# A hybrid decoder step on one core: group norm of a scan's head pair deferred into the next head pair, low parts of the weights split on VectorE, and the last matmul job cut in two halves

## The reference, cut to what matters

```python
# RWKV-7, 8 heads of 64; state S per head, one step per token:
S = S * decay + (S @ (-kk)) (kk * a) + v k      # outer products
y = S @ r
# then per head: group norm, bonus, gate
y = (y - mean(y)) / sqrt(var(y) + GN_EPS) * ln_g + ln_b
o = (y + sum(r * k * r_k) * v) * g
...
x = x + relu(x @ W_up) ** 2 @ W_down            # squared-ReLU MLP
y_out = rmsnorm(x, norm_final_g)
```

## Time and profile before

| | us |
|---|---|
| median of three runs | 1272.91 |
| the three runs | 1270.98, 1272.91, 1279.83 |
| the profiled execution's own time | 1272.74 |
| span of its trace, first to last instruction | 1271.1 |
| busy: PE, DVE, ACT, POOL | 1209.3, 661.1, 385.7, 181.3 |
| mean granted clock of TensorE | 0.986 |

### The profile page before, as it was taken

One profiled execution on the slowest core, in us unless ns is written; L12 is line 12 of the kernel. 1 busy time (PEld: TensorE's weight loads), 2 busy tenths in 40 slices (PEclk: granted clock), 3 DMA queues, 4 the chain that ended last, 5 costly groups with the idle time before them and its releaser, 6 DMA issues.

```text
span 1271.1 us, 26790 instructions
## 1 busy us (share of the span) xinstructions
PE 1209.3 (95%) x11356; PEld 1077.9 (85%) x11359; DVE 661.1 (52%) x1190; ACT 385.7 (30%) x743; POOL 181.3 (14%) x218
## 2 busy tenths in 40 slices
PE   7999999898999899889989999999999999999994
PEld 5777665585887888887888899999999999999994
DVE  4898778440634534544362466656554254354334
ACT  2211333343532334333333342233232122122121
POOL 0414000111442242231142200000000000000000
PEclk9999999999999999989999999999999999999997
DMA  8234533233101111201211156522222222222101
GB/s 309 80 121 151 166 114 133 80 137 117 35 19 61 60 53 62 102 11 60 96 68 36 45 189 221 199 96 71 92 75 100 80 87 101 70 97 100 67 34 71
DMA packets 39178, 122.82 MB, mean 97 GB/s; under 512 B 5282, under 2 KB 16546, under 8 KB 30482
## 3 DMA queue, kind: packets, MB, share of 16 engines
q1 hardware_dynamic: 37106, 116.01, 26.2%
q0 software_dynamic: 1952, 5.09, 1.2%
HBM read 109.18 MB, written 11.90 MB: 95 GB/s over the span
## 4 chain that ended last, share of the span: by engine, by line
PE 86%; DVE 7%; issue 2%; ACT 2%; POOL 1%; DMA 1%; SPq 0%; DVEq 0%; ACTq 0%; POOLq 0%
PE ps L1540 13%; PE ps L1543 13%; PE ps L1539 13%; PE ps L989 7%; PE ps L980 5%; PE ps L947 5%; PE ps L981 3%; PE ps L982 3%; PE ps L1283 2%; PE ps L1107 2%; PE ps L1334 1%; PE ps L987 1%; PE ps L984 1%; PE ps L1371 1%; PE ps L1347 1%
## 5 line engine op out<-in xcount | busy, mean ns | idle before, releaser
L563 ACT ACTIVATE wh<-land 128x1024 fp32r<-128x1024 f32 (+1 forms) x125 | 122.1, 977 | 360.3 <-PE ps L1543 360.3
L571 DVE TENSOR_TENSOR wl<-land,wh 128x1024 fp32r<-128x1024 f32 (+1 forms) x94 | 103.3, 1099 | 149.7 <-ACT wh L563 149.0
L980 PE MATMUL ps<-xghi,wh 128*128 128x272 f32 x464 | 151.6, 327 | 9.8 <-ACT R L1652 8.5
L1539 PE MATMUL ps<-xhi,wh 128*128 128x272 f32 x512 | 138.3, 288 | 0.0
L1540 PE MATMUL ps<-hl,wh 128*128 128x272 f32 x512 | 138.2, 289 | 0.0
L1540 PE MATMUL ps<-xlo,wh 128*128 128x272 f32 x512 | 138.2, 289 | 0.0
L1539 PE MATMUL ps<-hh,wh 128*128 128x272 f32 x512 | 138.1, 288 | 0.0
L981 PE MATMUL ps<-xlo,wh 128*128 128x272 f32 x464 | 135.1, 291 | 0.0
L982 PE MATMUL ps<-xghi,wl 128*128 128x272 f32 x464 | 134.9, 291 | 0.0
L980 PEld LDWEIGHTS ps<-xghi,wh 128*128 128x128 f32 x464 | 88.9, 192 | 23.6 <-issue 14.3
L1543 PE MATMUL ps<-xhi,wl 128*128 128x272 f32 x512 | 106.1, 288 | 0.0
(11 more groups left out here) (436 smaller groups left out, 2390.5 us busy)
## 6 DMA issues: line engine op xcount, KB each, us to landing
land<-in_slabs SPq DMA_DIRECT2D x51, 1024.0 KB, 4.8
ring<-in_slabs SPq DMA_DIRECT2D x14, 1024.0 KB, 5.4
gates<-R SPq DMA_DIRECT2D x24, 272.0 KB, 2.1
merge<-gates SPq DMA_DIRECT2D x24, 272.0 KB, 2.9
land<-in_slabs SPq DMA_DIRECT2D x12, 512.0 KB, 5.0
R<-in_kv SPq DMA_DIRECT2D x24, 128.0 KB, 2.0
pb<-in_kv SPq DMA_DIRECT2D x24, 128.0 KB, 2.0
xT<-in_xT SPq DMA_DIRECT2D x4, 544.0 KB, 6.9
```

The lines of the kernel that those rows point to most:

```text
L563: act.activation(hi, src, ACT.Copy).then_inc(s["weights_hi"], 1)
L571: dve.tensor_tensor(lo, src, hi.bitcast(F32), ALU.subtract).then_inc(s["weights_lo"], 1)
L980: pe.matmul(ps[:, b, 0:HALF], whi[:, k], hi, start=a, stop=False)
L1539: pe.matmul(ps[:, b + h, 0:HALF], whi[:, k], hi[k][:, c], start=a, stop=False)
```

## The change

1. **Group norm of pair j is deferred.** Its mean wide is put into prep of pair j+1 behind the first fill place, its centring on DVE behind that; the square on ACT and the var wide come before chunk 0 of j+1; the square root on ACT in chunk 0; reciprocal, product, scale and shift, and gate on DVE in the chunks 2, 3, 5 and 6; the gate's wide in chunk 5. Only pair 3's stays in the old place. The outputs `y_` and the bonus have buffers for each pair.
2. **Pair j+1 is begun earlier.** `ahead(j+1, 0..2)` (token mix, scan, subtractions) goes into chunk 7 and dec of pair j, the exponentials to ACT in dec, `factors(j+1)` on DVE behind the last step of dec. The differences of r are issued early on POOL.
3. **`early_lo` goes from POOL's queue to DVE's**, one behind a chunk's state or in dec, prep and gn.
4. **Budgets**: prep 5, 5, 4, 4 instead of 8, 8, 6, 8; a chunk 2, 3, 3 instead of 2, 2, 2 (5 in two places); dec 5 each; pair 3's gn 9, 13, 15. The total stays.
5. **The last down job is done one half after the other** (`split_by_half`), so that the first half's norm can start while the second is multiplied. The sum over features gives 68 partitions x 4 columns (`end_sum`, 68x1 matmuls), on which root and reciprocal are taken; `end_spread` brings it back to 128 partitions. The stores go out as four DMAs a half.
6. Small ones: a different order of the branch sources' splits, the copy of y ahead of an eviction in chunk 7, `fill("dec", j, 1)` ahead of the inverse's second step.

```diff
@@ fill_plan
-        waits += [(("prep", j, n), b) for n, b in zip((0, 1, 3, 2), (8, 8, 6, 8) if j else (8, 22, 10, 8))]
+        waits += [(("prep", j, n), b) for n, b in zip((0, 1, 3, 2), (5, 5, 4, 4) if j else (8, 22, 10, 8))]
...
-        waits += [(("chunk", NCH * j + c, n), 5 if (c, n) == (NCH - 1, 2) else 2) for c in range(NCH) for n in range(3)]
-        waits += [(("dec", j, n), 4) for n in range(5)]
-        waits += [(("gn", j, n), b) for n, b in enumerate((6, 6, 10))]
+        waits += [(("chunk", NCH * j + c, n), (5 if j and c == 4 else 2, 3, 5 if c == NCH - 1 else 3)[n]) for c in range(NCH) for n in range(3)]
+        waits += [(("dec", j, n), 5) for n in range(5)]
+    waits += [(("gn", 3, n), b) for n, b in enumerate((9, 13, 15))]
@@ early_lo
-        def early_lo(pool, n):
-
-            pool.wait_ge(s["weights_hi"], n - PARTS0 + 1)
+        def early_lo(dve, n):
+
+            dve.wait_ge(s["weights_hi"], n - PARTS0 + 1)
             src, hi, lo = split_views(n)
-            pool.tensor_tensor(lo, src, hi.bitcast(F32), ALU.subtract).then_inc(s["early_lo"], 1)
+            dve.tensor_tensor(lo, src, hi.bitcast(F32), ALU.subtract).then_inc(s["early_lo"], 1)
@@ PE, prep
                 else:
                     fill("prep", j, 0)
-                fill("prep", j, 1)
-                fill("prep", j, 3)
+                    pe.wait_ge(s["s_y_out"], j)
+                    wide(0, k_("blk"), y_[j - 1]).then_inc(s["mean"], 1)
+                    fill("prep", j, 1)
+                    pe.wait_ge(s["sstate"], j)
                 pe.wait_ge(s["rk"], j + 1)
                 wide(6, k_("blk"), L_).then_inc(s["rk_sum"], 1)
+                if j:
+                    fill("prep", j, 3)
+                    pe.wait_ge(s["yc"], j)
                 fill("prep", j, 2)
                 if j < 3:
                     fill("need", "pb", 9 + j)
-                if j:
-                    pe.wait_ge(s["oB_out"], j)
@@ PE, chunks
+                if j:
+                    pe.wait_ge(s["yc_sq"], j)
+                    wide(0, k_("blk"), var_[j - 1]).then_inc(s["var"], 1)
                 for c in range(NCH):
...
+                    if j and c == 0:
+                        fill("chunk", n, 2)
+                        pe.wait_ge(s["y_rt"], j)
                     if j < 3 and c in (0, 1, 3):
                         early(j + 1, (0, 1, 0, 2)[c])
-                    fill("chunk", n, 2)
+                    if j and c == 5:
+                        if j < 3:
+                            pe.wait_ge(s["kk_rt"], j + 2)
+                        wide(0, lora[:, 512 + P * (j - 1):512 + P * j], t13).then_inc(s["g"], 1)
+                    if not (j and c == 0):
+                        fill("chunk", n, 2)
@@ PE, dec
+                fill("dec", j, 1)
                 pe.wait_ge(s["s_inv_out"], 4 * j + 2)
                 for hh, hp, hs in HEAD:
                     mm = pe.matmul(ps[hs, 7, 0:NS], ssq[hs], sx[hs], start=True, stop=True)
                 mm.then_inc(s["s_inv"], 1)
-                fill("dec", j, 1)
@@ PE, last job
+            split_by_half(NJOB - 1, H[1], 0, range(KT))
+            split_by_half(NJOB - 1, H[1], 1, range(0, 3))
+            pe.wait_ge(s["norm_rt"], 3)
+            end_sum(0)
+            split_by_half(NJOB - 1, H[1], 1, range(3, 6))
+            end_spread(0)
+            split_by_half(NJOB - 1, H[1], 1, range(6, KT))
+            end_sum(1)
+            end_spread(1)
@@ ACT, chunk 0
                     evacs("chunk", n, 1)
+                    if j and c == 0:
+                        act.wait_ge(s["var"], j)
+                        act.activation(h2(var_[j - 1]), pair(0), ACT.Sqrt, bias=gneps, scale=1.0 / 64).then_inc(s["y_rt"], 1)
                     if j < 3 and c < 4:
                         early(j + 1, c)
@@ DVE, chunks and dec
+                    if c:
+                        for m in splits(("chunk", n - 1)):
+                            early_lo(dve, m)
                     if j < 3 and c < 7:
                         early(j + 1, c)
+                    if j and c in (2, 3, 5, 6):
+                        group_norm(j - 1, (0, 0, 1, 2, 0, 3, 4)[c])
+                    if j < 3 and c == NCH - 1:
+                        ahead(j + 1, 0)
+                        ahead(j + 1, 1)
...
+                if j < 3:
+                    ahead(j + 1, 2)
+                for n in splits(("chunk", NCH * j + NCH - 1), ("dec", j, 0)):
+                    early_lo(dve, n)
                 dve.wait_ge(s["s_inv"], 2 * j + 1)
...
+                if j < 3:
+                    factors(j + 1)
+                    dve.wait_ge(s["sstate"], j + 1)
+                    dve.tensor_copy(sdec, tA[:, SEQ + 3:TOK:4])
+                for n in splits(("dec", j, 2), ("dec", j, 4)):
+                    early_lo(dve, n)
@@ DVE, end
+            end_add(0)
+            end_inverse(0)
+            end_scale(0, range(0, 2))
+            end_add(1)
+            end_scale(0, range(2, 5))
+            end_inverse(1)
+            end_scale(0, range(5, KT))
+            end_scale(1, range(KT))
```

More of the change, by code:

```diff
@@ L290, in split_tags @@
         tags += [("chunk", NCH * j + c, 2) for c in range(NCH)]
-        tags += [("dec", j, n) for n in (0, 2, 4)] + [("gn", j, n) for n in (1, 2)]
+        tags += [("dec", j, n) for n in (0, 2, 4)]
+    tags += [("gn", 3, n) for n in range(3)]
     order = {tag: n for n, tag in enumerate(FILLS)}
@@ L480, in build @@
         AR, bt, kt_, tA, tB = cut(R, 8 * TOK, 2, TOK), slot[10], slot[11], slot[12], slot[13]
-        y_ = r_
+        y_ = [pb3[:, 4 + j, 0:TOK] for j in range(3)] + [r_]
+        bonus = [pb3[:, 8 + j, 0:TOK] for j in range(3)] + [L_]
+        kka = k__
+        var_ = [L_, L_, r_, tA]
         G = 14 * TOK
@@ L846, in _ @@
             diff(v__, 8)
+            pool.wait_ge(s["t12"], 2)
+            diff(r_, 0)
             for j in range(4):
-                if j:
[L849 to L852, removed]
                 if j == 0:
@@ L888, in _ @@
                     diff(v__, 9 + j)
+                    pool.wait_ge(s["factors"], j + 1)
+                    diff(r_, j + 1)
                 if j == 0:
@@ L1576, in _ @@
                 split_step(up0 + n, X, ks)
-            for n in range(up0 + 2, NJOB):
+            for n in range(up0 + 2, NJOB - 1):
                 kind, idx, *_ = JOBS[n]
@@ L1834, in _, with exps @@
             evacs("c", 4)
+            def exps(j):
+                act.wait_ge(s["lx"], j + 1)
+                act.activation(tA, L_, ACT.Exp).then_inc(s["exps"], 1)
+                act.activation(tB, L_, ACT.Exp, scale=-1.0).then_inc(s["exps"], 1)
+                act.activation(lw, a_, ACT.Exp).then_inc(s["exps"], 1)
+                act.activation(scf, scf, ACT.Exp).then_inc(s["exps"], 1)
             for j in range(4):
@@ L1952, in _ @@
                         square(3, xT3, TOK, idx - 25)
-            norm(3, xT3, TOK, KT - 1)
+            end = evacuated(NJOB - 1, "v")
+            for h in range(2):
+                c = slice(h * HALF, (h + 1) * HALF)
+                act.wait_ge(s["evac_v"], end + h)
+                act.wait_ge(s["norm_ss"], KT * 4 - 2)
+                act.activation(nbuf[3][0][:, (KT - 1) % 2, c], xT3[:, KT - 1, c], ACT.Square).then_inc(s["norm_sq"], 1)
+                act.wait_ge(s["norm_sum"], 3 + 2 * h)
+                act.activation(endt[0:QT, 4 * h:4 * h + 4], ps[0:QT, 4 + h, 0:4], ACT.Sqrt, bias=epsc[0:QT],
+                               scale=1.0 / D).then_inc(s["norm_rt"], 1)
         @block.vector
@@ new lines, in _ @@
+            for n in range(3, 7):
+                early(0, n)
+            for n in range(3):
+                ahead(0, n)
+            factors(0)
+            for j in range(4):
+                if j:
+                    group_norm(j - 1, 0)
+                dve.wait_ge(s["rk_sum"], j + 1)
+                dve.tensor_tensor(h2(bonus[j]), pair(6), h2(v__), ALU.mult).then_inc(s["bonus"], 1)
+                if j == 0:
+                    dve.tensor_copy(sdec, tA[:, SEQ + 3:TOK:4])
+                    early_lo(dve, PARTS0)
+                    early_lo(dve, PARTS0 + 1)
@@ L2280, in _ @@
                                       mask_bc, ALU.mult).then_inc(s["m4"], 1)
+                for n in splits(("prep", j)):
+                    early_lo(dve, n)
                 for r in range(1, 4):
@@ L2392, in _ @@
             inverse(2, TOK)
-            for n in range(job_at("up", 0), NJOB):
+            for n in range(job_at("up", 0), NJOB - 1):
                 kind, idx, *_ = JOBS[n]
```

231 lines of the change are left out of this document (143 added, 88 removed).

## The result

| | before | after |
|---|---|---|
| median, us | 1274.55 (6 runs, 1270.98 to 1279.83) | 1254.78 (6 runs, 1253.59 to 1258.55) |
| the profiled execution, us | 1272.74 | 1254.46 |
| its span, us | 1271.1 | 1252.8 |
| mean granted clock | 0.986 | 0.993 |

The ratio is 0.985 with a 95% interval of 0.983 to 0.9869: faster by 1.5%, 19.8 us between the medians. The forecast was 1253 us. Between the two profiled executions the sum had 19.4 us less, and 18.3 came.

The account below looks back on a forecast made before the run. PE, busy 95% of the span, was taken as the bound, leaving its waits to gain: from 1272.74 us, 28.8 removed, 16.4 added, 7.0 less at the end gave 1253 us, range 1243 to 1262.

Parts of the forecast that it names:

- (a): Boundaries between two pairs: PE's idle time and slower clock in three stretches go, 23.4 us less.
- (b): A chunk of pair 2: the late state behind a POOL low part, with its clock fall, goes, 3.2 us less.
- (c): Start of dec, three times: the wait goes as the copy of y moves ahead of an eviction, 2.2 us less.
- A1: First fill step behind the mean wide, three times: waits 1.6 us for a low part on DVE, 4.8 us more.
- A2: The inverse in dec: four uncovered waits of about 0.5 us and smaller ones at other steps, 2.7 us more.
- A3: Chunks 0 and 1: u waits behind the tanh's table load, 1.8 us for pairs 1 and 2, 3.9 us more altogether.
- A4, A5: Chunk ends with the z copy queued on ACT, 1.4 us more; chunk 4 of pair 0 on DVE, 0.2 us more.
- A6: PE's clock behind the new waits: two falls taken out of five long waits, 3.4 us more, bounds 0 to 8.5.
- the end: Behind the last matmul 9.7 us instead of 18.2, with 1.5 more inside the last job: 7.0 us less.
- DVE as the bound: Rival: DVE bounds the chunk loop at the state's scaling, 1287 us at 1.2 us per chunk; chance 0.03.
- the boundary did not stay: Rival: PE still stands at the pairs, only the end and a part gained, 1266 to 1269 us; chance 0.07.
- The clock at each new wait: Rival: all five long waits of A1 and A3 bring a clock fall, 1258.4 us; chance 0.14.

Follow-up runs that it names:

- e6: Changed kernel with dec's low part put ahead of the next pair's factors on DVE; 1253.55 us, ratio 0.983.
- e2: Changed kernel with the next pair's mix, scan, exponentials and factors back in prep, norm still deferred; 1267.74 us, ratio 0.9958.
- e1: Changed kernel with the low parts back on POOL, all else kept; 1262.01 us, ratio 0.9904.
- e5: Changed kernel with a one-column tanh behind the deferred norm's root in pairs 1 and 2, loading the tanh's table early; 1249.89 us, ratio 0.9806.
- e3: Changed kernel with the last job, final norm and stores as before the change; 1258.95 us, ratio 0.9886.
- e4: Changed kernel with 15 of the low parts, those between chunk states, computed twice on DVE; 1259.08 us, ratio 0.9879.
- e7: Changed kernel with dec's second fill place dealt three steps ahead of the inverse's second step and two behind; 1256.53 us, ratio 0.9857.
- e8: Changed kernel with the three edits of e5, e6 and e7 together; 1248.06 us, ratio 0.9788.
- e9: Changed kernel with the edits of e5 and e6, dec's fill steps back behind the inverse's second step, and DVE's order in dec changed; 1245.39 us, ratio 0.9771.

## Why the prediction was right

The time was forecast within 2 us, and most terms by place and size. Against the profiled executions, in us:

| term | forecast | measured | from |
|---|---|---|---|
| (a) boundaries | -23.4 | -22.0 | idle 15.4 gone; three stretches at lower clock, 1.6, 3.4 and 1.6 |
| (b) chunk of pair 2 | -3.2 | -3.2 | no such wait |
| (c) start of dec | -2.2 | -2.2 | no such wait |
| A1 | +4.8 | +4.1 | 3 x 1.35, after against e6; the waits show 3 x 1.1 |
| A2 | +2.7 | +2.3 | 4 x 0.58 |
| A3 | +3.9 | +3.5 | 2 x 1.76 |
| A4, A5 | +1.6 | +1.6 | 5.5 less 3.5, less the 0.4 of before |
| A6 clock | +3.4 | +3.4 | two falls, both at A3 |
| the end | -7.0 | -5.0 | 11.0 + 2.2 against 18.2 |
| sum | -19.4 | -17.5 | the spans: -18.3 |

That the sums agree so closely has some luck in it. What (a) and the end give back was taken 3.4 us too high, and A1 to A3 cost 1.5 us less than was taken, so that the errors work against each other. The stretch up to the scan was 1.4 us shorter, of which 0.7 is a wait for a load, and another 0.6 us or so stand against it that no row names.

*The mechanism of (a)* is shown for the early start: with it undone (e2), the wait for the factors comes back at all three boundaries. Its size was taken too high, because the work was counted as bare matmuls; each change between scan and fill steps costs PE a little more (the 0.49 us of the fill step behind the wide in the earlier trace rows against 0.29 inside a run), and that stays. No run undoes the norm's deferral alone, or the budgets alone; what each of them does to the boundaries is argued from the order of the queues. (b) and (c) went, but no run takes them apart either, and that (b) went because the low parts left POOL is not shown: in e1 they are back there, and no chunk's state is late.

*A1* was too high by 0.2 us a place: DVE's chain took 5.9 us from dec's last matmul, not 6.1, and PE's ten steps 3.86, not 3.73. e6 shows the cause by taking it away. The 1.09 us that the profile shows as the wait are less than it cost, because they are counted from the end of the wide's record, 1.08 us behind its start, while a step that does not wait starts 0.72 behind it.

*A3* was right, and e5 shows that the table load behind the wide was the cause.

*The end* is the mis-sized term. Behind the last matmul it was 11.0 us in place of 9.7: eight scales, not eleven, were still to be done, but the way there (half an addition and square, the sum, the root, the reciprocal and the spread) took 4.7 us, where 1.9 and 0.7 and three half scales had been taken. The spread alone took 1.88, at half clock, for 1.11 in other traces. And 1.0 us of the 18.2 before was a slower clock as well, as e3 shows, so that the halves as such are worth 4.1, with the 0.8 us of the slow spread counted against them. Inside the job the small matmuls cost 2.2 us, where 1.5 had been taken.

*A6* was right by count. It could easily not have been: the choice of two falls out of five rests on the two waits of before that the prediction set side by side, and the runs show no such regularity, below. *The rivals*: DVE as the bound falls by e4; the boundary did not stay; the waits were not half as long. The clock at each new wait came at A3 and not at A1.

## What to carry to other kernels

Before moving work between two queues, list for each place what stands ahead on the new queue and how long the other engine's cover is: nearly every new wait here came out of such a sum within half a microsecond. A wait is priced with the clock that may fall behind it, and an activation of one column that calls the next function's table early can be worth more than the wait it shortens. An operation that was deferred brings its table load, its queue place and its cover with it, so the places that it lands in are where to look next: some 10 us more were there.

## What the runs showed of the hardware that was not expected

The same wait does not always cost the same. TensorE's wait of 1.76 us before the u of chunk 1 of pair 1 stands in after, e1, e2 and e4, with the same matmuls ahead of it. In e2 the clock behind it stayed at 1.00; in after TensorE ran at half clock, 1.2 GHz, for 3.3 us; in e1 and e4 for some 10 us. The row is of e2, the others stand above.

```profile
460.00:475.00 15.00, 13.21 (x130) 10.82 (x130) 4.05 (x9) 7.64 (x13) 0.00 (x0) 1.00 0.08 30
```

With pair 2's, and with e3, e6 and e7, there are 14 such waits in seven traces: behind one there was no fall, behind eight 3.4 us at half clock, and behind five 10.2. The wait of 2.05 us at the norm ahead of the MLP had a fall in six of the thirteen traces, e8 (0.89) among them, and none in e5, e9 and after. So executions of one kernel differ by steps of 1.7 to 5 us, and a gain of that size has to be read from waits in the trace or from a kernel in which the wait itself is gone. The Trainium skill's page "TensorE: Matmul & The Clock Gate", section "HAM oscillation — how this bites in real kernels", describes a loop in which every wait for data, longer ones than these, is followed by a throttled burst; here some waits are and some are not, with the wait and the work the same.

An operation of DVE that has both inputs outside PSUM can be held by one of POOL's until that ends, however short it is: 0.18 us became 2.19 in e1, and 2.1 or more in all four pairs' dec, while the one that reads PSUM kept its 0.17 us beside the same subtraction.
